# Pool mixing as three rounded products, cut by token thirds, with a weight ring of six places

## The reference

```
z      = rms_norm(x) @ w_in_pool                # u (1536) | gate (1536) | memory query (512) | memory gate (512)
u_ext  = 15 rows of history, then u             # zeros for the prompt, state_pool for the samples
pooled = mean of the last w tokens of u_ext - u # 4 groups of 384 channels, w = 2, 4, 8, 16
mixed  = pooled[g] @ w_grp[g]                   # 384 x 384 for each group g
branch = mixed * pool_scale                     # then branch * silu(gate), beside memory attention, @ w_out
new_pool_state = last 15 rows of u_ext
```

## Time and profile before

| | us |
|---|---|
| median of 3 runs | 2331.04 (2330.99 to 2335.4) |
| profiled execution, its own time | 2338.4 |
| its span | 2336.7 |
| PE busy | 2201.2 (94%) |
| DVE busy | 1292.6 (55%) |
| ACT busy | 1009.2 (43%) |
| POOL busy | 433.0 (19%) |

### The profile page before, as it was taken

One profiled execution on the slowest core, in us unless ns is written; L12 is line 12 of the kernel. 1 busy time (PEld: TensorE's weight loads), 2 busy tenths in 40 slices (PEclk: granted clock), 3 DMA queues, 4 the chain that ended last, 5 costly groups with the idle time before them and its releaser, 6 DMA issues. The chain is left out here.

```text
span 2336.7 us, 47103 instructions
## 1 busy us (share of the span) xinstructions
PE 2201.2 (94%) x18709; PEld 1834.6 (79%) x18709; DVE 1292.6 (55%) x2040; ACT 1009.2 (43%) x2090; POOL 433.0 (19%) x542
## 2 busy tenths in 40 slices
PE   7799999997999689999999998889999999998999
PEld 6799899886688589999999997766666566654787
DVE  6846666435422374334444443588888888875211
ACT  7533223215311144333333343457777777775100
POOL 0533223202000043222222221321121111100000
PEclk9899999998899889999999999889999999999999
DMA  8222222144635553334433336789999999978331
GB/s 289 86 87 89 79 64 66 66 166 163 210 119 155 146 186 102 109 99 133 153 106 109 96 96 234 253 292 379 396 407 393 406 395 388 375 284 307 123 108 55
DMA packets 283274, 453.98 MB, mean 194 GB/s; under 512 B 30962, under 2 KB 208062, under 8 KB 283038
## 3 DMA queue, kind: packets, MB, share of 16 engines
q1 hardware_dynamic: 274958, 421.83, 51.8%
q0 software_dynamic: 8000, 29.10, 3.3%
q10 hardware_dynamic: 96, 0.02, 0.0%
HBM read 372.43 MB, written 78.43 MB: 193 GB/s over the span
## 5 line engine op out<-in xcount | busy, mean ns | idle before, releaser
L233 DVE TENSOR_TENSOR h_w_lo<-l_w,h_w_hi 128x512 fp32r<-128x512 f32 x264 | 213.7, 811 | 221.2 <-ACT h_w_hi L226 218.7
L226 ACT ACTIVATE h_w_hi<-l_w 128x512 fp32r<-128x512 f32 x264 | 166.7, 633 | 239.9 <-PE i_c L322 81.4
L320 PE MATMUL i_x<-h_t_hi,h_w_hi 128*128 128x264 f32 x560 | 163.3, 292 | 6.8 <-DVE h_t_lo L279 6.8
L2960 PEld LDWEIGHTS b_krow<-ar_arena,b_qd 128*32 128x32 f32 x3072 | 107.2, 111 | 72.6 <-issue 57.0
L192 POOL TENSOR_TENSOR h_w_lo_full<-l_w 128x512 f32<-128x512 f32 x44 | 57.5, 1308 | 560.5 <-DMA l_w<-in_w_in_sb_dram 229.9
L320 PE MATMUL i_y<-h_t_hi,h_w_hi 128*128 128x264 f32 x560 | 161.3, 288 | 0.0
L322 PE MATMUL i_x<-h_t_hi,h_w_lo 128*128 128x264 f32 x560 | 161.0, 287 | 0.0
L321 PE MATMUL i_x<-h_t_lo,h_w_hi 128*128 128x264 f32 x560 | 160.4, 286 | 0.0
L321 PE MATMUL i_y<-h_t_lo,h_w_hi 128*128 128x264 f32 x560 | 159.0, 284 | 0.0
L322 PE MATMUL i_y<-h_t_hi,h_w_lo 128*128 128x264 f32 x560 | 158.9, 284 | 0.0
L2960 PE MATMUL b_krow<-ar_arena,b_qd 128*32 128x128 f32 x3072 | 140.7, 279 | 7.9 <-ACT b_kev L2666 6.9
(11 more groups left out here) (368 smaller groups left out, 6424.9 us busy)
## 6 DMA issues: line engine op xcount, KB each, us to landing
ar_arena<-in_cache_sb_k_dram SPq DMA_DIRECT2D x73, 768.0 KB, 9.7
bf_vpage<-in_cache_sb_v_dram SPq DMA_DIRECT2D x64, 768.0 KB, 8.8
b_vpage<-in_cache_sb_v_dram SPq DMA_DIRECT2D x64, 768.0 KB, 8.5
l_w<-in_w_in_sb_dram SPq DMA_DIRECT2D x56, 512.0 KB, 3.9
l_w<-in_cache_sb_k_dram SPq DMA_DIRECT2D x36, 768.0 KB, 9.4
l_w<-in_w_in_pool_dram SPq DMA_DIRECT2D x32, 512.0 KB, 4.2
bf_kpage<-in_cache_sb_k_dram SPq DMA_DIRECT2D x19, 768.0 KB
ar_arena<-scratch_yT SPq DMA_DIRECT2D x14, 1024.0 KB, 6.6
```

Source lines behind the costliest of these rows:

```text
L226: act.activation(self.w_hi[:, i % RING, :, :], self.source(i), ACT.Copy).then_inc(self.high, 1)
L233: dve.tensor_tensor(self.w_lo[:, i % RING, :, :], self.source(i), self.w_hi[:, i % RING, :, :].bitcast(F32), ALU.subtract).then_inc(self.r ...
L320: pe.matmul(out, w_hi, t_hi, start=kk == 0 and x in ("P1", "P2", "P5"), stop=False, skip_group_check=True)
L2960: ins = pe.matmul(krow[pair * CT:(pair + 1) * CT, 0:P], qd[:, i % 2, at:at + CT], kt[u % 2][:, h, f, :], start=odd == 0 and f == 0, stop=o ...
```

## The change

The mixing products are made of three rounded passes, with `up` and `wg` split into high and low parts; thirds of tokens are outermost; third 0 stands between P1 and P2, thirds 1 and 2 between P2 and P6; `turn_state` stands behind P6. To find room, the ring of layer 0 has six places (the two spare ones hold `wg_hi` and `tail`), the sum buffers double as `up_hi`, and head 0 of `qT` is loaded after the last mixing product. Layer 1 keeps eight places.

```diff
@@ class Quads
+        self.ring = PLACES if i else PLACES - 2
+        self.ahead = self.ring - 1
...
+    def slot(self, i):
+        return PLACES - self.ring + i % self.ring
@@ front_phase, scalar
-                for j in range(3):
+                for j in range(2):
                     q.round(act, j)
                 key_root(1)
                 evacuate(7)
-                q.round(act, 3)
                 act.wait_ge(s["made"], 14)
-                for j in range(4, 6):
+                for j in range(2, 6):
                     q.round(act, j)
@@ front_phase, vector
-                for j in range(3):
+                for j in range(2):
                     q.remainder(dve, j)
                 key_normed(1)
                 evacuate(7)
                 first_sum(7)
+                q.remainder(dve, 2)
                 other_sums(7)
@@ MemoryAhead
+        self.parts = 2 - i
...
-            gp.wait_ge(self.ql, 16)          # in pad
+            gp.wait_ge(self.ql, 16 * self.parts)
@@ pool_phase, sync
                     for m in range(GB):
-                        sp.wait_ge(s["mixed"], 9 * n + 3 * m + 3)
+                        sp.wait_ge(s["mixed"], 9 * n + 7 + m)
                         sp.dma_start(S["yT0"][g * GB + m], gate[:, m, :])
...
-                memory.queries(sp)
+                memory.queries(sp, 1, MH)
+                memory.scales(sp)
+                sp.wait_ge(s["mready"], 9 * GROUPS)
+                memory.queries(sp, 0, 1)
                 memory.own_keys(sp)
                 finish_group(GROUPS - 1)
@@ pool_phase, scalar
+                def mix_weights(n):
+                    act.wait_ge(s["wgl"], 16 * (n + 1))
+                    if n:
+                        act.wait_ge(s["mready"], 9 * n)
+                    for kk in range(GB):
+                        act.activation(wg_hi[kk], wg[:, kk, :], ACT.Copy).then_inc(s["wgh"], 1)
+                def mix_high(n):
+                    act.wait_ge(s["pooled"], GB * (n + 1))
+                    for u in range(NT):
+                        if u >= 2:
+                            act.wait_ge(s["mready"], 9 * n + 3 * (u - 1))
+                        act.activation(up_hi[u % 2], up[:, :, HIST + u * TT:HIST + (u + 1) * TT], ACT.Copy)
...                                                # in the P4 block, behind the Silu instructions
+                        for n in range(1, GROUPS):
+                            if p + 1 == first(n):
+                                mix_high(n - 1)
                         if p + 1 < q.n:
                             begin(p + 1)
+                    # mix_weights(n) at (first(n) + 1, "P6"); mix_high(GROUPS - 1) at the end
@@ pool_phase, vector
+                def mix_low(n, u):
+                    dve.wait_ge(s["uph"], NT * n + u + 1)
+                    dve.tensor_tensor(up_lo[:, :, cols], up[:, :, cols], up_hi[u % 2].bitcast(F32), ALU.subtract)
                 def mix(n):
+                    mix_low(n, 0)
+                    mix_low(n, 1)
                     dve.wait_ge(s["tailt"], n + 1)
...
-                    for m in range(GB):
-                        for u in range(NT):
+                    for u in range(NT):
+                        if u == 1:
+                            mix_low(n, 2)
+                        for m in range(GB):
+                    # mix_weights(n) (three subtractions) at (first(n) + 1, "P6"); history(n) at P3, was P6
@@ pool_phase, tensor
+                def group(n, thirds):
+                    pe.wait_ge(s["wgr"], GB * (n + 1))
+                    for u in thirds:
+                        pe.wait_ge(s["upr"], NT * n + u + 1)
+                        for m in range(GB):
...
-                                ins = pe.matmul(aux[(at + 1) % 2][:, 0:TT], wg[:, kk, m * P:(m + 1) * P], ...)
+                                ins = product3(pe, aux[(at + 1) % 2][:, 0:TT], wg_hi[kk][:, rows], wg_lo[:, kk, rows],
+                                               up_hi[u % 2][:, kk, :], up_lo[:, kk, cols], kk == 0, kk == GB - 1)
...
                         if n and (p, x) == (first(n), "P1"):
-                            group(n - 1)
-                        if (p, x) == (first(n), "P2"):
+                            group_tail(n - 1)
+                            group(n - 1, range(1))
+                        if n and (p, x) == (first(n), "P2"):
+                            group(n - 1, range(1, NT))
+                        if (p, x) == (first(n), "P6"):
                             turn_state(n)
```

More of the change, by code:

```diff
@@ L88 @@
 K2 = KD // 2
-RING, AHEAD = 8, 7
+PLACES = 8
 class Quads:
@@ L188, in combine @@
         if x == "P5":
-            if i >= RING:
-                gp.wait_ge(self.done, 2 * (i - RING) + 2)
+            if i >= self.ring:
+                gp.wait_ge(self.done, 2 * (i - self.ring) + 2)
             gp.wait_ge(self.loaded_b[p % 2], 16 * (p // 2 + 1))
-            gp.tensor_tensor(self.w_full[:, i % RING, :, :], a21, a22, ALU.add).then_inc(self.combined, 1)
+            gp.tensor_tensor(self.w_full[:, self.slot(i), :, :], a21, a22, ALU.add).then_inc(self.combined, 1)
         if x == "P1":
@@ L217, in round @@
         p, x = self.seq[i]
-        if i >= RING:
-            act.wait_ge(self.done, 2 * (i - RING) + 2)
+        if i >= self.ring:
+            act.wait_ge(self.done, 2 * (i - self.ring) + 2)
         if x in ("P1", "P2"):
@@ L1017, in pool_phase, with two_kinds @@
         first = lambda n: 4 + 3 * n
-        wg = k.sb("wg", [P, GB, GW])
-        up = k.sb("up", [P, GB, HIST + T])
+        def two_kinds(name, shape):
+            full = k.sb(name, shape)
+            size = 4 * shape[1] * (shape[2] if len(shape) == 3 else 1)
+            return full, nc.alloc_sbuf_tensor_at(f"p_{name}_r", shape, F32R, offset=nc.sbuf_base - size)
+        wg, wg_lo = two_kinds("wg", [P, GB, GW])
+        up, up_lo = two_kinds("up", [P, GB, HIST + T])
         us = k.sb("us", [P, GB, NB_S, SX])
-        sums = [k.sb(f"sum{i}", [P, EXT]) for i in range(2)]
+        sums, up_hi = zip(*(two_kinds(f"sum{i}", [P, GB * TT]) for i in range(2)))
+        up_hi = [a[:, :].rearrange("p (k t) -> p k t", k=GB) for a in up_hi]
+        spare = lambda ring: ring[:, 0:PLACES - q.ring, :, :].rearrange("p r k n -> p (r k n)")
+        wg_hi = [spare(q.w_hi)[:, 0:GW], spare(q.w_hi)[:, GW:2 * GW], spare(q.w_lo)[:, 0:GW]]
         ssum = [k.sb(f"ssum{i}", [P, NB_S, SX]) for i in range(2)]
@@ L1070, in _ @@
                 for i, (p, x) in enumerate(q.seq):
-                    q.loads(sp, i + AHEAD - 1)
+                    q.loads(sp, i + q.ahead - 1)
                     if x == "P4" and p < 4:
@@ L1114, in _ @@
                 gp.memset(up[:, :, 0:HIST], 0.0).then_inc(s["zeroed"], 1)
-                for j in range(6, AHEAD + 1):
+                for j in range(6, q.ahead + 1):
                     q.combine(gp, j)
                 for i, (p, x) in enumerate(q.seq):
-                    q.combine(gp, i + AHEAD + 1)
+                    q.combine(gp, i + q.ahead + 1)
                     if (p, x) in ((0, "P4"), (1, "P4")):
@@ L1150, in begin @@
                     q.copy(act, p, "P5", part(p, 1, 1), ACT.Copy)
+                def mix_weights(n):
[9 more added lines that the diff above has]
+                            act.wait_ge(s["mready"], 9 * n + 3 * (u - 1))
+                        act.activation(up_hi[u % 2], up[:, :, HIST + u * TT:HIST + (u + 1) * TT], ACT.Copy
+                                       ).then_inc(s["uph"], 1)
                 q.tokens_scalar(act, 0)
-                for j in range(6, AHEAD):
+                for j in range(6, q.ahead):
                     q.round(act, j)
                 for i, (p, x) in enumerate(q.seq):
-                    q.round(act, i + AHEAD)
+                    if i + q.ahead >= 6:
+                        q.round(act, i + q.ahead)
                     kind_a, _, kind_b, _ = POOL_KINDS[p]
@@ L2105, in _ @@
                     q.token_fetch(sp, S["tok"], t)
-                for j in range(AHEAD - 1):
+                for j in range(q.ahead - 1):
                     q.loads(sp, j)
                 for i, (p, x) in enumerate(q.seq):
-                    q.loads(sp, i + AHEAD - 1)
+                    q.loads(sp, i + q.ahead - 1)
                     kind, h = kinds[p]
@@ L2142, in _ @@
             def _(gp):
-                for j in range(AHEAD + 1):
+                for j in range(q.ahead + 1):
                     q.combine(gp, j)
                 for i, (p, x) in enumerate(q.seq):
-                    q.combine(gp, i + AHEAD + 1)
+                    q.combine(gp, i + q.ahead + 1)
                     if (p, x) in ((0, "P4"), (1, "P4")):
```

70 lines of the change are left out of this document (42 added, 28 removed).

## The result

The changed kernel takes 2343.63 us (median of five runs, 2340.98 to 2347.23) against 2331.04 (2329.28 to 2335.4) for the kernel before beside it: a ratio of 1.0044, interval 1.0029 to 1.0058. The forecast was 2333, its range 2325 to 2339. A second timing of both gave 2342.06 (12 runs) against 2331.72 and a ratio of 1.0039, interval 1.0027 to 1.0051: some 9 us slower. Slow runs (over 1.5% above the fastest of the same kernel) are left out of every ratio.

The account below looks back on a forecast made before the run. PE, busy 94% of the span, was taken as the bound, held up at five places. Front - 0.2, mixings - 6.3, clock + 1.5 and hand-over + 6.8 made + 1.8 us on the median 2331.04: 2333, range 2325 to 2339.

Parts of the forecast that it names:

- The hand-over, + 6.8: Layer 0 to memory attention: later last product, loads and stores delay the memory phase by 6.8 us (5.9 to 8.8).
- The last product: Last group's mixing at the hand-over: done after 18.4 us, against 16.4 before.
- The wait of 4.5 us: Before the last group's third 0: PE waits for Silu 2.1, rounding 1.1 and subtraction 1.3 us.
- From the first store to the landing: Tail stores at the hand-over: issued from 515.2, landed at 521.3, between 520.3 and 523.3.
- rival B: Hand-over is serial: loads and stores take turns, + 9.7 or more instead of 6.8; 2336 to 2339 us, chance 0.2.
- The memory phase was to move with the tail: Start of memory attention: key pages are issued at the tail's landing, so the phase moves + 6.8 us.
- The mixings and the first pair, - 6.3 + 1.5 - 2.0: Layer 0: three mixings between pairs save 6.3 us, half clock costs 1.5, first pair wins back 2.0.
- POOL's sum: First mixing alone: the sum for the next P5 slows a neighbouring DVE step, 1.0 us (0 to 2.2).
- The front, - 0.2: Front phase ends 1.8 us later, the first pair wins 2.0 back: together - 0.2 us.
- C: Six-place ring starves PE behind each mixing or at group 0's pooling: some 3 us at three places, 2342, chance 0.07.
- D: Mixing passes no faster: pitch 0.233, 18.9 us a mixing, four cost 11 us more than before; 2344, chance 0.03.
- A: Hand-over absorbed by slack in the memory phase: only PE's 2 us lateness counts, - 4.5 in all, 2326, chance 0.2.

Follow-up runs that it names:

- last_plain: Changed kernel with its last group mixed as before (unrounded, tile by tile, stores between, queries and own keys after the last product): 2329.04 us, ratio 0.9982.
- round_early_last: Changed kernel with ACT rounding thirds 0 and 1 of the last group before it copies P4: 2337.56 us, ratio 1.0015.
- filled_wait: Changed kernel with 36 unread transposes on PE in the wait before the last group's third 0: 2341.97 us, ratio 1.0038.
- stores_by_third: Changed kernel with the last group's tail stores ahead of the mixing and y stored as each third is mixed: 2333.49 us, ratio 1.0017.
- best: last_plain with all thirds behind P2, the state's DMA a pair earlier and P1 copied before P5 behind a mixing: 2324.18 us, ratio 0.9956.
- state_ahead: Kernel before the change with only the DMA of the state rows asked for a pair earlier: 2327.06 us, ratio 0.9973.
- before: Kernel before the change, unedited, first profile: profiled execution 2338.4 us, median of runs 2331.04 us.
- before_again: Kernel before the change, unedited, profiled a second time: profiled execution 2328.8 us, ratio against itself 1.0013.
- ring_six: Kernel before the change with only six places in layer 0's ring and the new front-phase order: 2334.97 us, ratio 1.0000.
- turn_late: Kernel before the change with only the state's turning moved behind P6 and the history copy to P3: 2325.16 us, ratio 0.9964.
- after: Changed kernel, unedited, first profile: profiled execution 2344.01 us, median of runs 2343.63 us, ratio 1.0044.
- after_again: Changed kernel, unedited, second profile and timing: profiled execution 2345.3 us, median 2342.06 us, ratio 1.0039.
- turn_early: last_plain with the state's turning back behind P2 and the history copy back at P6: 2345.68 us, ratio 1.0057.

## Why the prediction was wrong

*The hand-over, + 6.8, is the step that failed.* In the two profiles of the changed kernel it takes 114.9 and 115.0 us; in the nine with the last group mixed as before it takes 99.7 to 103.9, 102.2 in the mean. So it costs 12.8, and last_plain says 13.0 in the time. That the end of the phase moves with the landing of the tail was right. Two things in the term were not: the half clock behind stops was left out of it, twice, and the stores land later than I took. 2.1 + 1.1 + 2.8 us, as follows, make 12.8 out of 6.8:

- The last product was to be done 18.3 us behind the start of the transposes and was at 20.4 (SP's issue of head 0 at 504.96, less 484.52): 2.1 us later. The wait of 4.5 us was right (4.45); that PE then runs two thirds of third 0 at the lower level, some 2.2 us, was left out. I had put the clock's price at the mixings, where it didn't fall, and none at the longest stop of the change. round_early_last takes wait and clock away together, filled_wait the clock alone (18.3).
- From the first store to the landing I took 6.1 us (5.1 to 8.1); it was 7.25 (514.26 - 507.01), 1.1 more. With both, the fourth key page is issued 29.7 us behind the transposes, against 19.8 before: + 10, rival B's number, but by a late product and by stores that overlap in part, not by five transfers in turn.
- The memory phase was to move with the tail, and up to the transposes of the fourth page it does: they start 33.5 us behind the last group's transposes, against 23.9 in the earlier trace rows (+ 9.6). From there to the end it is 2.9 us longer than in the mean of the nine. The time line says where: PE has waited 1.8 us for this page, just after the 6.2 us at the end of the block, and runs its transposes and the scores behind them at the lower level, 0.8 and 2.0 us more than at the full clock; after that the phase takes as long as in the nine. (The whole phase is 88.3 us against 83.0, since it also starts 2.1 to 2.5 us earlier in relation to the page.) stores_by_third has the same long stop at the end of the block and none before this page, and its scores keep the clock:

```profile
512.51 5.35 PE L1605 MATMUL a_bank<-c_ident,l_w 128*128 128x128 f32 x24 [6.44 <-PEq L76]
517.65 1.43 PE L1605 MATMUL a_bank<-c_ident,a_more 128*128 128x128 f32 x8
519.91 1.93 PE L1615 MATMUL a_bank<-a_mkT,mp_qpad 128*32 128x256 f32 x32 [0.83 <-ACT a_mkT L1491]
```

round_early_last and filled_wait, which still wait for the page (1.7 and 1.0 us), lose the clock at the scores. So the second wait goes with these 2.8 us. It is read from rows, not tested alone: in best a wait of 1.37 us for the page left the clock at its full level, in state_ahead one of 1.38 did not. Nor was head 0 put back to its old place by itself.

*The mixings and the first pair, - 6.3 + 1.5 - 2.0, were right in sum, partly by luck.* From the first product to the last transposes the profiles that mix as before with the early turning (before, before_again, ring_six) took 401.3, 394.6 and 398.6 us, and the changed kernel 391.3 twice: - 6.9 on the mean, against - 6.8. But I set the terms against one execution that had lost the clock at two boundaries of three. Against one that lost it nowhere the gain is 3.3. In the rows: a pitch of 0.16, right; stretches after the first of 22.8 against 23.5 (23.1 and 23.4 in the second profile), since the state is there sooner than I thought; the first 24.1 against 24.5. At the first one third 0 starts 2.00 us behind the transposes' start, at the other two 1.55: POOL's sum, for which I charged 1.0, cost 0.45: the pooling step of 32 elements beside it took 1.29 us in place of 0.18, but ACT's Silu covered most of that. P6 waits 1.65 us, as worked out. No clock was lost there: 1.5 too much. So a saving set too high against a long profile, a state that came early and a clock that held cancel each other.

*The front, - 0.2.* The first product of layer 0 starts at 92.8 us in the mean of four profiles with the old order and at 94.2 in ten with the new: + 1.4 against + 1.8. From there to the first mixing about 1 us comes back, half of the 2.0.

*The rivals.* C (the ring of six) is ruled out by ring_six, D (no faster passes) by the pitch; D's own sum was wrong as well, for 11 us more than before in place of 12.2 less is 23 us above the forecast, some 2356 and not 2344. A (absorbed) is wrong by its sign. B had the right side and the right landing of the tail; at 2339 at most it was still 3 to 5 us short, for it too ended at the tail and had no clock in it.

*What I did not ask.* The passes save 3 us of matmuls at a boundary, and pay 1.1 to 1.7 us before third 0 and 1.65 before P6, waits that unrounded products don't have, and at the first mixing 0.7 for the state. turn_late shows that this sum is below nothing: its three stretches take 67.1 us, those of the changed kernel 69.7. The whole gain of the three boundaries was the later turning's. I compared the change with the kernel before, never with the half of it that was free.

## What to carry to other kernels

Where a change has several parts, sum the cheapest part alone as well: here a transfer asked for sooner, or its reader moved behind one product, gave 0.3 to 0.4%. With the recast of the arithmetic around it 0.2% was left (last_plain), and with the last group recast as well the kernel was 0.4% slower. A faster operation that first needs its operands prepared belongs where other work covers the preparing; where nothing covers it, as at the end of a block, prepare earlier (round_early_last won 5.6 us) or leave the slow form (last_plain won 13). And price a new stop of several us with the half clock behind it, from a row that has one.

## What the runs showed of the hardware

A kernel whose PE stops for some 2 us at a boundary lost the granted clock there in one execution and not in another, and the length of the stop alone does not tell which. In the first profile of before the stops are 2.15, 2.66 and 1.92 us and the stretches have 1.00, 0.94 and 0.93; in the second they are 1.53 to 1.59 us and all have 1.00; in ring_six a stop of 2.53 us kept 1.00 and one of 1.80 had 0.93. Stops of 4 us and more brought the level of 1.2 GHz in every profile that had them: 3.97 us before third 0 in after, after_again and stores_by_third, 4.63 to 5.60 us ahead of P6 in turn_early, 6.2 to 6.4 us at the end of the block in the five profiles with the changed hand-over. 36 transposes that nobody reads, in place of a stop of 3.97 us, kept the clock at 0.98. And one issuer's DMAs queue: a store of 528 KB issued 0.5 us behind a load of 512 KB and 0.9 behind one of 528 KB was over after 6.4 us, against 2.7 in the median of the others.
